# A hybrid encoder block in two-part float32: the order of high and low matmul runs in pairs of wide units

## The chip, the cores and the metric

The kernel runs on one core of a Trainium2 chip. The time is the device time of one execution in microseconds; beside it stands the span of one profiled execution.

## The reference, cut to what matters

```python
u = rmsnorm(h, g_mix)
z = u @ w_in                       # q, k, v, latents, gates: 512 tokens x 2048, one matrix
...                                # two attention branches, gated, merged, projected
gu = rmsnorm(h, g_ffn) @ w_gate_up # 2048 -> 2 x 5632
h = h + (silu(gate) * up) @ w_down # 5632 -> 2048
...                                # a second gate, an embedding, a last norm
```

All of it is float32. The change is about three of these products: part of the first matrix, gate and up, and down.

## The kernel before

**Two parts.** TensorE works on float32 in a rounded form. Each operand is split into a high part (the rounded value, a copy on ScalarE) and a low part (the rest, a subtraction on VectorE). A product is high x high, high x low and low x high. The weights' high part multiplies both parts of the activations (the high run), the weights' low part only the high part (the low run).

**Seven products in place of eight.** The three matrices are multiplied by a scheme of the Strassen-Winograd kind. The work is cut into units `v` of 128 output columns for each of the two halves; each unit has seven products, `j` = 0 to 6 (B11, T1, T4, B21, T2, B22, T3), with eight weight tiles of 128x128 each (`pairs(v)`, six in the last units). The first matrix has 10 such units, gate and up has `FF` = 44, down has 24; gate, up and down are numbered through as 68 units. Units go in pairs, a = 2q and b = 2q + 1, and their products alternate: (a,0), (b,0), (a,1), (b,1) and so on. `order(v, j)` is that position. I call the two products of one j a step.

**Wide units.** In a narrow unit the high run is 16 matmuls of 256 columns (two for each weight tile), the low run eight of 256. In a wide unit (`wide(v)`, `z_wide(v)`) one matmul of 512 columns takes the place of the two: eight of 512, then eight of 256. Wide are pairs q = 1 to 20 of gate and up, four pairs in down (q = 23, 24, 27, 28) and q = 1 to 3 of the first matrix.

**The weights' ring.** The split weights of product n lie in slot n modulo 3 of `S_HI` and `S_LO`. ScalarE's copy for n waits until product n - 3 is done, whose slot it takes, and VectorE's subtraction for n waits for that copy:

```python
act.wait_ge(s_used, n - 2)          # hi(n) on ScalarE
copy(S_HI[ring(n)][:, columns(v)], operand(v, j)).then_inc(s_hi, 1)
dve.wait_ge(s_hi, n + 1)            # lo(n) on VectorE
tt(S_LO[s][:, columns(v)], operand(v, j), S_HI[s][:, columns(v)], ALU.subtract).then_inc(s_lo, 1)
```

TensorE raises `s_used` at the end of each low run, and waits for `s_hi` before the high run and `s_lo` before the low run. In the first matrix the same semaphores are called `z_used`, `z_hi` and `z_lo`.

**What is emptied when.** A unit has four banks of PSUM, which a and b of the next pair use again (a after a, b after b). ScalarE copies partial results out (`snap_s1`, `snap_row`, `snap_s2`); VectorE adds the last ones: `gate_sum(u)` after product 5 (line 2706), `up_sum(u)` after product 6 (line 2728), the latter the one for which product 0 of unit u + 2 waits. In down the adds are `add` (line 2774), in two halves for a wide unit: `add_c11_c12` after product 5, and `add_u3` after product 6, for which the next pair waits. In the first matrix they are `z_first_sum` (line 2219) and `z_second_sum` (line 2226).

**The order on VectorE** is written out by hand, t = 0 to 13 for the 14 products of a pair, `lo(14q + t + 2)` at each t. The end of a pair in gate and up is:

```python
# t = 11: lo(b,6), t_2, gate_sum(a)
# t = 12: lo(next a,0), t_4, gate_sum(b)
# t = 13: up_sum(a), lo(next b,0)
# t =  0: up_sum(b), lo(next a,1)
```

`t_2` and `t_4` are small subtractions on hidden values (lines 2762 and 2766). The copy of ScalarE is line 1311 for every use. The loads of raw weights (SyncE's queue) wait for `s_lo` and `s_sum`, and POOL adds one block onto another with a DMA.

Of the kernel before, what the change touches and what calls it, by code (L numbers as in the profile page):

```python
# [89 lines left out]
BANK_OF = (ALPHA, GAMMA, DELTA, BETA, ALPHA, GAMMA, ALPHA)  # L90


def pairs(v):

    return 6 if v >= FF + 16 else 8


def generation(v):

    return 0 if v < FF else 1 + (v - FF) // 8  # L100


def first_unit(g):

    return 0 if g == 0 else FF + 8 * (g - 1)


def bank0(v):

    return 4 * ((v + 1) % 2)  # L110


def order(v, j):

    return 14 * (v // 2) + 2 * j + v % 2


def wide(v):

    q = v // 2  # L120
    return 0 < q < FF // 2 - 1 if v < FF else q < FF // 2 + 8 and (q - FF // 2) % 4 in (1, 2)
# [30 lines left out]
def snap_at(u, which):  # L152

    return 6 * (u // 2) + ((1, 2, 5), (3, 4, 6))[u % 2][which]


def ff_sum_at(u, which):

    return 4 * (u // 2) + 2 * which + u % 2 + 1
# [7 lines left out]
def added_at(v, which):  # L167

    return sum(10 * weight(2 * q) for q in range(FF // 2, v // 2)) + weight(v) * (2 * which + v % 2 + 1)
# [4 lines left out]
def z_wide(v):  # L174

    return 0 < v // 2 < Z_UNITS // 2 - 1
# [7 lines left out]
def z_slot(v, i):  # L184

    return ((7, 4, 5, 2), (6, 0, 1, 3))[v % 2][(i - v // 2) % 4]


def z_ring(n):

    return (n + 2) % 3
# [10 lines left out]
def build(nc, xT, pT, gains, tables, mats, w_in, w_z, w_qb, w_kvb, w_a, w_b, w_o, w_gu, w_dn, w_dn6, w_pg, w_pp,  # L202
          outT):
    with ExitStack() as ctx:
# [42 lines left out]
        ps = ctx.enter_context(nc.psum_tensor("ps", [P, 8, SEQ], F32))  # L247
# [68 lines left out]
        def flat(slot):  # L316
            return slot.rearrange("p t k c -> p (t k c)")
# [4 lines left out]
        def ff_pair(g):  # L322
            return (g - G_E + 2) % 4
# [38 lines left out]
        S_HI = [flat(w_hi[:, 0]), flat(w_hi[:, 1]), hi_2[:]]  # L362
        S_LO = [flat(w_lo[:, 0]), flat(w_lo[:, 1]), lo_2[:]]
        E_HI, E_LO = ([of[i] for i in (2, 1, 0, 1)] for of in (S_HI, S_LO))

        def as_4_by_256(slot):
            return slot.rearrange("p (t k c) -> p t k c", t=2, k=KP)
# [4 lines left out]
        def ring(n):  # L372
            return (1, 0, 2)[n % 3]
# [6 lines left out]
        def x_slot(g, j):  # L380
            s, n = (7 * g + j) % 8, 6 if g == 3 else 8
            a = arena[:, 4 * s:4 * s + 4].rearrange("p u t c -> p (u t c)")
            return a[:, 0:n * 512].rearrange("p (t k c) -> p t k c", t=2, k=n)

        X_HALF = [slice(0, 256), slice(256, 512)]
# [18 lines left out]
        def z_operand(v, j):  # L404

            return RAWS[z_slot(v, (A11, A21, A22, A12, A21, A12, A22)[j])]
# [6 lines left out]
        def z_tile(j, k):  # L413
            if j == B11_:
                return r0[:, k, :, X_HALF[0]]
            if j == B21_:
                return r1[:, k, :, X_HALF[0]]
            if j == B22_:
                return r1[:, k, :, X_HALF[1]]
            return z_turned(j)[:, :, k]  # L420
# [409 lines left out]
        def _(pe):  # L830
# [135 lines left out]

            rotary_key_group()

            def z_product(v, j):
                n = order(v, j)  # L970
                if v < 2 and j == 0:
                    pe.wait_ge(u_lo, 16)
                if v == 0:
                    if j == 1:
                        pe.wait_ge(rstd_done, 1)
                    if j == 2:
                        pe.wait_ge(kr_parts, 1)
                    if j in (T1_, T4_, T2_, T3_):
                        pe.wait_ge(zx_lo, {T1_: 2, T4_: 4, T2_: 6, T3_: 8}[j])
                elif v == 1:  # L980
                    if j < 2:
                        pe.wait_ge(emptied, j + 1)
                elif j == 0:
                    pe.wait_ge(z_acc, ff_sum_at(v - 2, UP_SUM))
                if j >= 4:
                    pe.wait_ge(z_snap, snap_at(v, j - 4))
                pe.wait_ge(z_hi, n + 1)
                bank = ps[:, bank0(v) + BANK_OF[j]]
                hi, lo = S_HI[z_ring(n)], S_LO[z_ring(n)]
                both = z_wide(v)  # L990
                fresh = j < 4
                out = bank[:, X_HALF[1 if both else 0]]
                parts = bank.rearrange("p (t c) -> p t c", t=2)
                for k in range(8):
                    w, x = hi[:, k * P:k * P + P], z_tile(j, k)
                    if both:
                        mm(parts, w, x, start=fresh and k == 0, stop=False, skip_group_check=not fresh)  # L997
                    else:
                        mm(out, w, x[:, 0], start=fresh and k == 0, stop=False, skip_group_check=not fresh)  # L999
                        mm(out, w, x[:, 1], start=False, stop=False, skip_group_check=not fresh)  # L1000
                pe.wait_ge(z_lo, n + 1)
                for k in range(8):
                    i = mm(out, lo[:, k * P:k * P + P], z_tile(j, k)[:, 0], start=False, stop=k == 7,  # L1003
                           skip_group_check=not fresh)
                i.then_inc(z_used, 1)

            for a in range(0, Z_UNITS, 2):
                for j in range(7):
                    z_product(a, j)
                    z_product(a + 1, j)  # L1010

            def first_value():
                pe.wait_ge(v_in, 16)
# [163 lines left out]
            hi, lo = as_4_by_256(S_HI[2]), as_4_by_256(S_LO[2])  # L1177
# [3 lines left out]
            i.then_inc(piece_used, 1)  # L1181


            def strassen(v, j):
                n = order(v, j)
                if j == 0 and v == 1:
                    pe.wait_ge(emptied, G_E)
                elif j == 0 and v >= 2:
                    if v < FF + 2:
                        pe.wait_ge(ff_sum, ff_sum_at(v - 2, UP_SUM))  # L1190
                    else:
                        pe.wait_ge(added, added_at(v - 2, ADD_U3))
                if j == 3 and v == 1:
                    pe.wait_ge(log_done, 4)
                    pe.wait_ge(refine, 10)
                if j >= 4:
                    if v < FF:
                        pe.wait_ge(snap, snap_at(v, j - 4))
                    else:
                        pe.wait_ge(added, added_at(v, j - 4))  # L1200
                g = generation(v)
                if v == 0:
                    pe.wait_ge(xs_lo, (7, 8, 14, 14, 15, 16, 17)[j])
                elif g and v == first_unit(g):
                    pe.wait_ge(fill_lo, 14 * (g - 1) + 2 * j + 2)
                pe.wait_ge(s_hi, n + 1)
                x, bank = x_slot(g, j), ps[:, bank0(v) + BANK_OF[j]]
                hi, lo = S_HI[ring(n)], S_LO[ring(n)]
                both = wide(v)
                fresh = j < 4  # L1210
                out = bank[:, X_HALF[1 if both else 0]]
                parts = bank.rearrange("p (t c) -> p t c", t=2)
                for k in range(pairs(v)):
                    if v == 0 and k == 6 and j >= 2:
                        pe.wait_ge(xs_lo, (18, 19, 20, 21, 22)[j - 2])
                    w = hi[:, k * P:k * P + P]
                    if both:
                        mm(parts, w, x[:, :, k], start=fresh and k == 0, stop=False, skip_group_check=not fresh)  # L1218
                    else:
                        mm(out, w, x[:, 0, k], start=fresh and k == 0, stop=False, skip_group_check=not fresh)  # L1220
                        mm(out, w, x[:, 1, k], start=False, stop=False, skip_group_check=not fresh)  # L1221
                pe.wait_ge(s_lo, n + 1)
                for k in range(pairs(v)):
                    i = mm(out, lo[:, k * P:k * P + P], x[:, 0, k], start=False, stop=k == pairs(v) - 1,  # L1224
                           skip_group_check=not fresh)
                i.then_inc(s_used, 1)

            pe.wait_ge(op_lo, OP_B + OPS_B * HEADS)
            for a in range(0, UNITS, 2):
                for j in range(7):  # L1230
                    strassen(a, j)
                    strassen(a + 1, j)
                    if a == 0 and j == 2:
                        total(3, 1)

# [2 lines left out]
            for g in range(8):  # L1238
# [5 lines left out]
                hi, lo = (of[g // 2].rearrange("p (k c) -> p k c", k=2) for of in (E_HI, E_LO))  # L1244
                c = [slice(256 * (g % 2) + P * t, 256 * (g % 2) + P * t + P) for t in range(2)]
                out = [ps[:, 2 * ff_pair(G_E + g) + t, :] for t in range(2)]
# [755 lines left out]
        def _(dve):  # L2002
# [333 lines left out]
            def seam_rotate(m, tile, before):  # L2336
                _, r, out = spare(m)
                dve.wait_ge(hnorm, m + 1)
                rotate(m, tile, 0, out, r, HD // 2, 2 * m + 2, before)
                dve.wait_ge(roped, m + 1)  # L2340
# [862 lines left out]
```

## Time and profile before

| | us |
|---|---|
| median of 3 runs (2646.85 to 2647.05) | 2646.94 |
| span of the profiled execution | 2645.5 |
| TensorE busy | 2630.8 |
| VectorE busy | 2019.1 |
| ScalarE busy | 1284.6 |

The span is one profiled execution from its first to its last instruction. In the trace a matmul stands with its full passage, so matmuls that follow each other overlap; the distance between two starts is what one costs. In a timeline row "x8" is a run of eight, and the number in brackets at a row's end is the idle time of the engine before it and what ended it.

### The profile page before, as it was taken

To read this page: it belongs to the slowest core of one execution; us is meant where nothing else is said; L and a number is where in the kernel's file an instruction comes from. 1 tells how busy PE (TensorE), PEld (TensorE's weight loads), DVE (VectorE), ACT (ScalarE), POOL (GpSimd) and SP (SyncE) were. 2 spreads that over 40 slices of the span, in tenths; PEclk is the share of its full clock that TensorE was granted. 3 is DMA by queue.
4 is the path that set the end of the run, shared out by engine and by line. 5 is a ranking of instruction groups with operands and counts; after the bars stand their busy time and mean duration, and the time that the engine had idled before them with its cause. 6 is when DMAs were issued, how large, how long until landed. Compare 5 with 4: busy or idle time off the path is not lost.

```text
span 2645.5 us, 37943 instructions
## 1 busy us (share of the span) xinstructions
PE 2630.8 (99%) x14980; PEld 2307.9 (87%) x14980; DVE 2019.1 (76%) x2314; ACT 1284.6 (49%) x1609; POOL 178.6 (7%) x140
## 2 busy tenths in 40 slices
PE   9999999999999999999999999999999999999998
PEld 7989888888888888898888888888899898999887
DVE  8887777655565433488998999999899898898745
ACT  7545455434455233455545555554555353454543
POOL 0000000010000111100000000000000000000052
PEclk9999999999999999999999999999999999999999
DMA  7545423233333554446546555545666664653332
GB/s 252 154 143 169 123 87 96 80 91 119 98 100 103 183 210 124 145 127 177 166 144 178 168 158 173 175 138 166 175 198 213 211 211 140 207 140 106 94 101 99
DMA packets 135791, 392.75 MB, mean 148 GB/s; under 512 B 11600, under 2 KB 41424, under 8 KB 133072
## 3 DMA queue, kind: packets, MB, share of 16 engines
q1 hardware_dynamic: 119904, 342.27, 38.8%
q0 software_dynamic: 11232, 39.85, 8.5%
q10 hardware_dynamic: 4496, 8.44, 0.8%
q8 instruction: 109, 1.79, 0.3%
q14 instruction: 50, 0.41, 0.0%
HBM read 304.26 MB, written 46.40 MB: 133 GB/s over the span
## 4 chain that ended last, share of the span: by engine, by line
PE 97%; DVE 2%; ACT 1%; issue 0%; DMA 0%; DVEq 0%; ACTq 0%
PE ps L1218 23%; PE ps L848 23%; PE ps L1224 16%; PE ps L853 11%; PE ps L1220 4%; PE ps L1221 4%; PE ps L997 3%; PE ps L1003 3%; PE ps L837 1%; PE ps L835 1%; PE ps L836 1%; PE ps L918 1%; PE ps L1000 1%; PE ps L999 1%; PE ps L1250 1%; PE ps L907 0%
## 5 line engine op out<-in xcount | busy, mean ns | idle before, releaser
L1311 ACT ACTIVATE w_hi<-raw 128x1024 fp32r<-128x1024 f32 (+1 forms) x538 | 562.6, 1046 | 753.5 <-PE ps L1224 409.9
L848 PE MATMUL ps<-arena,w_hi 128*128 128x512 f32 x2704 | 647.6, 391 | 0.2 <-DVE res L2038 0.2
L848 PEld LDWEIGHTS ps<-arena,w_hi 128*128 128x128 f32 x2704 | 505.3, 188 | 108.7 <-issue 3.4
L1218 PE MATMUL ps<-arena,w_hi 128*128 128x512 f32 x1792 | 448.7, 392 | 0.0
L2586 DVE TENSOR_TENSOR w_lo<-raw,w_hi 128x1024 fp32r<-128x1024 f32 (+1 forms) x314 | 373.8, 1191 | 78.8 <-ACT w_hi L1311 77.3
L2026 DVE TENSOR_TENSOR w_lo<-raw,w_hi 128x1024 fp32r<-128x1024 f32 x172 | 219.1, 1275 | 224.5 <-ACT w_hi L1311 223.6
L1218 PEld LDWEIGHTS ps<-arena,w_hi 128*128 128x128 f32 x1792 | 322.3, 189 | 57.6
L1224 PEld LDWEIGHTS ps<-arena,w_lo 128*128 128x128 f32 x2468 | 332.3, 191 | 17.5
L1224 PE MATMUL ps<-arena,w_lo 128*128 128x256 f32 x2468 | 346.4, 283 | 0.0
L853 PE MATMUL ps<-arena,w_lo 128*128 128x512 f32 x1352 | 334.3, 389 | 0.0
L1311 ACT ACTIVATE hi<-raw 128x1024 fp32r<-128x1024 f32 (+1 forms) x182 | 189.6, 1042 | 243.4 <-PE ps L1224 212.8
L853 PEld LDWEIGHTS ps<-arena,w_lo 128*128 128x128 f32 x1352 | 253.8, 188 | 52.7
L1218 PE MATMUL ps<-arena,hi 128*128 128x512 f32 x896 | 224.4, 392 | 0.0
L2586 DVE TENSOR_TENSOR lo<-raw,hi 128x1024 fp32r<-128x1024 f32 (+1 forms) x156 | 186.1, 1193 | 43.6 <-ACT hi L1311 42.8
L1218 PEld LDWEIGHTS ps<-arena,hi 128*128 128x128 f32 x896 | 161.1, 189 | 28.8
L1224 PEld LDWEIGHTS ps<-arena,lo 128*128 128x128 f32 x1228 | 165.4, 191 | 8.8
L1224 PE MATMUL ps<-arena,lo 128*128 128x256 f32 x1228 | 172.3, 283 | 0.0
L1220 PE MATMUL ps<-arena,w_hi 128*128 128x256 f32 x676 | 166.3, 283 | 0.2 <-ACT res L1311 0.2
L1221 PE MATMUL ps<-arena,w_hi 128*128 128x256 f32 x676 | 166.2, 283 | 0.0
L3065 POOL DMA_DIRECT2D raw<-raw x68 | 59.0, 868 | 1218.5 <-DMA raw<-w_gu 785.9
L1220 PEld LDWEIGHTS ps<-arena,w_hi 128*128 128x128 f32 x676 | 129.7, 192 | 0.5 <-ACT res L1311 0.4
L1221 PEld LDWEIGHTS ps<-arena,w_hi 128*128 128x128 f32 x676 | 129.8, 192 | 0.1
(280 smaller groups left out, 3360.0 us busy)
## 6 DMA issues: line engine op xcount, KB each, us to landing
raw<-w_gu SPq DMA_DIRECT2D x174, 512.0 KB, 4.1
raw<-raw POOLq DMA_DIRECT2D x70, 512.0 KB, 7.7
raw<-w_in SPq DMA_DIRECT2D x68, 512.0 KB, 3.6
raw<-w_dn SPq DMA_DIRECT2D x64, 512.0 KB, 5.3
hid<-res SPq DMA_DIRECT2D x22, 1024.0 KB, 5.0
raw<-w_z SPq DMA_DIRECT2D x40, 512.0 KB, 5.4
raw<-w_o SPq DMA_DIRECT2D x32, 512.0 KB, 3.7
raw<-w_pg SPq DMA_DIRECT2D x32, 512.0 KB, 3.6
```

The costliest lines, as they stand in the source:

```text
L848: mm(ps[:, bank + t, :], w_hi[:, s, t, k], x[:, part, :], start=first and k == 0 and part == 0, stop=False)
L853: i = mm(ps[:, bank + t, :], w_lo[:, s, t, k], x[:, 0, :], start=False, stop=last and k == len(xs) - 1)
L997: mm(parts, w, x, start=fresh and k == 0, stop=False, skip_group_check=not fresh)
L1003: i = mm(out, lo[:, k * P:k * P + P], z_tile(j, k)[:, 0], start=False, stop=k == 7, skip_group_check=not fresh)
L1218: mm(parts, w, x[:, :, k], start=fresh and k == 0, stop=False, skip_group_check=not fresh)
L1220: mm(out, w, x[:, 0, k], start=fresh and k == 0, stop=False, skip_group_check=not fresh)
L1221: mm(out, w, x[:, 1, k], start=False, stop=False, skip_group_check=not fresh)
L1224: i = mm(out, lo[:, k * P:k * P + P], x[:, 0, k], start=False, stop=k == pairs(v) - 1, skip_group_check=not fresh)
L1311: return nc.scalar.activation(out, in_, ACT.Copy, scale=scale)
L2026: tt(w_lo[:, j % HL], raw[:, j], w_hi[:, j % HL], ALU.subtract).then_inc(w_lo_done, 1)
L2586: tt(S_LO[s][:, columns(v)], operand(v, j), S_HI[s][:, columns(v)], ALU.subtract).then_inc(s_lo, 1)
L3065: pool.dma_start(RAWS[into][:, columns(v)], RAWS[more][:, columns(v)], accum_op=ALU.add).then_inc(sum_1_in[v % 2], 16)
```

## The change

In a wide pair, products 1 to 5 of both units are regrouped: high run of a, high run of b, low run of a, low run of b. Products 0 and 6, and all narrow pairs, keep their order. No matmul, copy, subtraction or load is added or removed.

```diff
+def together(both, j):
+
+    return both and 0 < j < 6
...
-            def strassen(v, j):
+            def strassen_high(v, j):
                 n = order(v, j)
...
+            def strassen_low(v, j):
+                n = order(v, j)
+                lo, x = S_LO[ring(n)], x_slot(generation(v), j)
+                out = ps[:, bank0(v) + BANK_OF[j], X_HALF[1 if wide(v) else 0]]
                 pe.wait_ge(s_lo, n + 1)
                 for k in range(pairs(v)):
                     i = mm(out, lo[:, k * P:k * P + P], x[:, 0, k], start=False, stop=k == pairs(v) - 1,
-                           skip_group_check=not fresh)
+                           skip_group_check=j >= 4)
                 i.then_inc(s_used, 1)
...
             for a in range(0, UNITS, 2):
                 for j in range(7):
-                    strassen(a, j)
-                    strassen(a + 1, j)
+                    strassen_high(a, j)
+                    if not together(wide(a), j):
+                        strassen_low(a, j)
+                    strassen_high(a + 1, j)
+                    if together(wide(a), j):
+                        strassen_low(a, j)
+                    strassen_low(a + 1, j)
                     if a == 0 and j == 2:
                         total(3, 1)
```

The same is done to `z_product` of the first matrix, split into `z_product_high` and `z_product_low` and called in the same way with `z_wide(a)`.

TensorE, step 4 of a wide pair in gate and up, before (`hi`, `w_hi` are slots of the high parts, `lo`, `w_lo` of the low parts; the first four rows are unit a):

```order
L1218 MATMUL ps<-arena,hi 128x512 [waits s_hi,snap]
L1218 MATMUL ps<-arena,hi 128x512 x7
L1224 MATMUL ps<-arena,lo 128x256 [waits s_lo]
L1224 MATMUL ps<-arena,lo 128x256 x7
L1218 MATMUL ps<-arena,w_hi 128x512 [waits s_hi,snap]
L1218 MATMUL ps<-arena,w_hi 128x512 x7
L1224 MATMUL ps<-arena,w_lo 128x256 [waits s_lo]
L1224 MATMUL ps<-arena,w_lo 128x256 x7
```

The same place on TensorE in the changed kernel:

```order
L1233 MATMUL ps<-arena,hi 128x512 [waits s_hi,snap]
L1233 MATMUL ps<-arena,hi 128x512 x7
L1233 MATMUL ps<-arena,w_hi 128x512 [waits s_hi,snap]
L1233 MATMUL ps<-arena,w_hi 128x512 x7
L1244 MATMUL ps<-arena,lo 128x256 [waits s_lo]
L1244 MATMUL ps<-arena,lo 128x256 x7
L1244 MATMUL ps<-arena,w_lo 128x256 [waits s_lo]
L1244 MATMUL ps<-arena,w_lo 128x256 x7
```

The high run of b, with its waits, stands ahead of the low run of a, whose last matmul raises `s_used` for a. The low run of b ends the step as before.

VectorE at the end of a wide pair in gate and up, before, from the subtraction for (b,6) to up_sum of b:

```order
L2586 TENSOR_TENSOR w_lo<-raw,w_hi 128x1024 [waits s_hi]
L2762 TENSOR_TENSOR res<-res 128x256 [waits t_sum]
L2706 TENSOR_TENSOR res<-res,ps 128x1024 [waits s_used,snap]
L2586 TENSOR_TENSOR lo<-raw,hi 128x1024 [waits s_hi]
L2766 TENSOR_TENSOR res<-res 128x256 [waits t_sum]
L2706 TENSOR_TENSOR res<-res,ps 128x1024 [waits s_used,snap]
L2728 TENSOR_TENSOR res<-res,ps 128x1024 [waits s_used,snap]
L2586 TENSOR_TENSOR w_lo<-raw,w_hi 128x1024 [waits s_hi]
L2728 TENSOR_TENSOR res<-res,ps 128x1024 [waits s_used,snap]
```

In the changed kernel the same rows stand in the same order with the same waits, 25 lines further down in the code. The whole orders of VectorE and ScalarE are unchanged; only TensorE's is another.

## Rows read from the trace of the kernel before

**Rows 1.** The page, busy time of TensorE and VectorE.

```profile
PE 2630.8 (99%) x14980; PEld 2307.9 (87%) x14980; DVE 2019.1 (76%) x2314; ACT 1284.6 (49%) x1609; POOL 178.6 (7%) x140
```

**Rows 2.** Busy time in stretches: pair 9, and from lo (b,2) to lo (b,6).

```profile
core 0: us, PE busy (x) PEld busy (x) DVE busy (x) ACT busy (x) POOL busy (x), PEclk, DMA share, GB/s
1483.03:1522.14 39.11, 39.11 (x227) 34.41 (x225) 35.33 (x38) 19.79 (x22) 1.75 (x2) 1.00 0.56 162
1492.77:1515.11 22.34, 22.34 (x129) 19.66 (x128) 20.18 (x22) 12.93 (x15) 1.75 (x2) 1.00 0.54 141
```

**Rows 3.** Timeline of TensorE (start, us), first matmul of pairs 1 and 21.

```profile
1170.18 0.40 PE L1218 MATMUL ps<-arena,hi 128*128 128x512 f32 x1
...
1952.31 0.28 PE L1220 MATMUL ps<-arena,w_hi 128*128 128x256 f32 x1
```

**Rows 4.** Timeline of TensorE where one width follows itself.

```profile
61.77 1.12 PE L1003 MATMUL ps<-arena,lo 128*128 128x256 f32 x8
62.73 0.28 PE L999 MATMUL ps<-arena,w_hi 128*128 128x256 f32 x1
...
2503.46 3.79 PE L848 MATMUL ps<-arena,w_hi 128*128 128x512 f32 x16
2507.09 1.75 PE L853 MATMUL ps<-arena,w_lo 128*128 128x512 f32 x7
```

**Rows 5.** Timeline of TensorE, end of pair 9: (b,5), (a,6), next pair's (a,0).

```profile
1513.76 2.00 PE L1218 MATMUL ps<-arena,hi 128*128 128x512 f32 x8
...
1516.55 2.00 PE L1218 MATMUL ps<-arena,w_hi 128*128 128x512 f32 x8
...
1522.14 0.86 PE L1218 MATMUL ps<-arena,hi 128*128 128x512 f32 x3
```

**Rows 6.** Timeline of ScalarE there: copies for (b,6) and next (a,0).

```profile
1514.02 1.06 ACT L1311 ACTIVATE w_hi<-raw 128x1024 fp32r<-128x1024 f32 x1 [1.25 <-PE ps L1224]
1516.81 1.06 ACT L1311 ACTIVATE hi<-raw 128x1024 fp32r<-128x1024 f32 x1 [1.73 <-PE ps L1224]
```

**Rows 7.** Timeline of VectorE there, t_2 and t_4 left out.

```profile
1515.11 1.23 DVE L2586 TENSOR_TENSOR w_lo<-raw,w_hi 128x1024 fp32r<-128x1024 f32 x1 [0.24 <-ACT w_hi L1311]
...
1516.59 1.22 DVE L2706 TENSOR_TENSOR res<-res,ps 128x1024 f32<-128x1024 f32 x1
1517.91 1.22 DVE L2586 TENSOR_TENSOR lo<-raw,hi 128x1024 fp32r<-128x1024 f32 x1
...
1519.38 1.21 DVE L2706 TENSOR_TENSOR res<-res,ps 128x1024 f32<-128x1024 f32 x1
1520.52 1.22 DVE L2728 TENSOR_TENSOR res<-res,ps 128x1024 f32<-128x1024 f32 x1
```

**Rows 8.** Timelines of VectorE and TensorE at the end of pair 21.

```profile
1991.94 0.68 DVE L2728 TENSOR_TENSOR res<-res,ps 128x512 f32<-128x512 f32 x1
...
1992.67 0.39 PE L1220 MATMUL ps<-arena,hi 128*128 128x256 f32 x1
1992.89 0.28 PE L1221 MATMUL ps<-arena,hi 128*128 128x256 f32 x1
```

**Rows 9.** Timelines of VectorE and TensorE, end of pair 24, in down.

```profile
2105.42 1.41 DVE L2774 TENSOR_TENSOR res<-ps,res 128x512 f32<-128x512 f32 x2
2107.07 1.23 DVE L2586 TENSOR_TENSOR lo<-raw,hi 128x1024 fp32r<-128x1024 f32 x1 [0.24 <-ACT hi L1311]
2108.21 2.86 DVE L2774 TENSOR_TENSOR res<-ps,res 128x512 f32<-128x512 f32 x4
...
2111.30 0.28 PE L1220 MATMUL ps<-arena,hi 128*128 128x256 f32 x1
```

**Rows 10.** Timelines of VectorE and TensorE, end of pair 2, first matrix.

```profile
172.50 1.22 DVE L2219 TENSOR_TENSOR res<-res,ps 128x1024 f32<-128x1024 f32 x1
174.16 1.23 DVE L2196 TENSOR_TENSOR lo<-raw,hi 128x1024 fp32r<-128x1024 f32 x1 [0.44 <-ACT hi L1311]
...
176.43 1.22 DVE L2226 TENSOR_TENSOR res<-res,ps 128x1024 f32<-128x1024 f32 x1
...
178.39 0.40 PE L997 MATMUL ps<-arena,hi 128*128 128x512 f32 x1
```

More of the change, by code:

```diff
@@ L967, in _, with z_product_high @@
             rotary_key_group()
-            def z_product(v, j):
+            def z_product_high(v, j):
                 n = order(v, j)
@@ L988, in z_product @@
                 bank = ps[:, bank0(v) + BANK_OF[j]]
-                hi, lo = S_HI[z_ring(n)], S_LO[z_ring(n)]
+                hi = S_HI[z_ring(n)]
                 both = z_wide(v)
@@ L1000, in z_product, with z_product_low @@
                         mm(out, w, x[:, 1], start=False, stop=False, skip_group_check=not fresh)
+            def z_product_low(v, j):
+                n = order(v, j)
+                lo = S_LO[z_ring(n)]
+                out = ps[:, bank0(v) + BANK_OF[j], X_HALF[1 if z_wide(v) else 0]]
                 pe.wait_ge(z_lo, n + 1)
@@ L1008, in _ @@
                 for j in range(7):
-                    z_product(a, j)
-                    z_product(a + 1, j)
+                    z_product_high(a, j)
+                    if not together(z_wide(a), j):
+                        z_product_low(a, j)
+                    z_product_high(a + 1, j)
+                    if together(z_wide(a), j):
+                        z_product_low(a, j)
+                    z_product_low(a + 1, j)
             def first_value():
@@ L1207, in strassen @@
                 x, bank = x_slot(g, j), ps[:, bank0(v) + BANK_OF[j]]
-                hi, lo = S_HI[ring(n)], S_LO[ring(n)]
+                hi = S_HI[ring(n)]
                 both = wide(v)
@@ L1221, in strassen @@
                         mm(out, w, x[:, 1, k], start=False, stop=False, skip_group_check=not fresh)
+            def strassen_low(v, j):
+                n = order(v, j)
+                lo, x = S_LO[ring(n)], x_slot(generation(v), j)
+                out = ps[:, bank0(v) + BANK_OF[j], X_HALF[1 if wide(v) else 0]]
                 pe.wait_ge(s_lo, n + 1)
@@ L1224, in strassen @@
                     i = mm(out, lo[:, k * P:k * P + P], x[:, 0, k], start=False, stop=k == pairs(v) - 1,
-                           skip_group_check=not fresh)
+                           skip_group_check=j >= 4)
                 i.then_inc(s_used, 1)
```

## The prediction

> **What bounds the kernel now.** I read the page first: TensorE is busy 99% of the span [rows 1]. Then the busy times of one pair of wide units in the gate and up product: in its 39.11 us TensorE is busy for all of it at a granted clock of 1.00, its 2.4 GHz level, while VectorE is busy 35.33 us, ScalarE 19.79 us and the DMA engines 0.56 of the time [rows 2]. So TensorE's own stream sets the time and nothing makes it wait. From the first matmul of pair 1 to the first of pair 21 are 782.13 us [rows 3], which is 20 pairs of 39.11 us, or 280 products of 2.79 us. Each pair after the first takes the same time to a hundredth, so what I find at one pair counts for its like. But VectorE is 90% full, takes its work strictly as written, and hands TensorE a bank of PSUM at each pair's start. That hand-over is the place to look at.
>
> **The seams between runs.** A wide product is eight matmuls of 512 columns (high) and eight of 256 (low). Where only one width stands, 16 matmuls of 512 take 3.63 us, so 0.227 each, and eight of 256 take 0.96 us, so 0.120 each [rows 4]. Eight of each would be 2.774 us; a product takes 2.793. The other 0.02 us goes at the changes of width. The change turns high, low, high, low into high, high, low, low: two of four width changes go, once in each of five steps of a pair. Wide pairs are 20 in gate and up, 4 in down, 3 in the first matrix: 27 x 5 = 135 steps, 135 x 0.02 = 2.7 us gained. Instructions are neither added nor taken away, and each matmul keeps its size. Between nothing (the cost belongs to each run's start, whatever stood before) and twice that, I take the 2.7.
>
> The Trainium skill ("TensorE: Matmul & The Clock Gate", section "Back-to-back issue gap") gives a spacing of N/2.4 + 2.5 ns for an isolated matmul at full clock, by its own width alone. By that rule the regrouping would gain nothing, not 2.7 us; the rows show 227 and 120 ns where it gives 216 and 109, and a seam that it doesn't have, so I go by the rows.
>
> **What the regrouping makes later.** I call a pair's first unit a and its second b, T5, T6 and T7 the starts of its products 5 and 6 and of the next pair. In step 5 the product (a,5) used to end 2.79 us before T6, since all of (b,5) followed: 1513.76 against 1516.55 [rows 5]. Now only the low run of b follows, 8 x 0.120 = 0.96 us. So `s_used` for (a,5) comes 2.79 - 0.96 = 1.83 us later against T6 and T7. The ring has three slots, and (b,6) takes the one of (a,5). ScalarE is already waiting for it: its copy for (b,6) starts at 1514.02, 0.26 us after (a,5) ends, takes 1.06 us, and it idled 1.25 us before it [rows 6]. VectorE waits for that copy too: `lo` for (b,6) starts at 1515.11 after 0.24 us of idle time [rows 7]. Both start 1.83 us later.
>
> Behind this `lo` VectorE has, in order: t_2, gate_sum of a, `lo` for the next (a,0), t_4, gate_sum of b, and last up_sum of a, without which the next pair's first matmul may not write its bank. In [rows 7] gate_sum starts at 1516.59 and `lo` at 1517.91, 1.32 us later; the same work back to back is 1.14 us (1519.38 to 1520.52), so 0.18 us is an idle piece that can absorb. up_sum of a ends at 1520.52 + 1.22 = 1521.74, and TensorE starts the next pair at 1522.14 [rows 5]: a margin of 0.40 us. The delay passes it by 1.83 - 0.18 - 0.40 = 1.25 us.
>
> What a late hand-over costs beyond that is seen once, at the end of pair 21: up_sum ends at 1991.94 + 0.68 = 1992.62, the first matmul starts at 1992.67, and the second only 0.22 us after it, where 0.12 is usual, as the weights' load no longer lies beside another matmul [rows 8]. That is 0.05 + 0.10 = 0.15 us. So each of these junctions stalls TensorE 1.25 + 0.15 = 1.40 us; 20 of them are 28.0 us.
>
> **The same in the other two stages.** In down the chain is `lo` (b,6), two halves of an add, `lo` (a,0), four halves. Idle before `lo` is 0.24 us, 0.32 with the 0.08 by which back-to-back work overlaps in the rows (1.22 long, 1.14 apart); the last half ends at 2108.21 + 2.86 = 2111.07, and TensorE goes on at 2111.30 [rows 9]: 1.83 - 0.32 - 0.23 + 0.15 = 1.43 us, four times, 5.7 us. In the first matrix there is no t_2 or t_4: `lo` starts 1.66 us after the sum where 1.13 would do, so 0.53 is absorbed, and the last sum ends at 176.43 + 1.22 = 177.65 against 178.39 [rows 10]: 1.83 - 0.53 - 0.74 + 0.15 = 0.71 us, three times, 2.1 us.
>
> **Does VectorE reach `lo` (b,6) in time, and does anything else come late?** In steps 2 to 5 only the b copies come 1.83 us later. From `lo` (b,2) to `lo` (b,6) are 22.34 us with 20.18 us of work [rows 2]; both ends move by the same, so 2.2 us of room stays. Going through the list with the work back to back, I find VectorE waiting again before `lo` (b,5), 0.9 us, and before `lo` (b,6), 1.2 us, so it is there when the copy is. TensorE now wants the high part of b earlier: copy (b,j+1) ends 0.26 + 1.06 us after (a,j), that is 0.36 us into the next step, and the high run of b begins 1.84 us into it: 1.5 us to spare. Low parts stay 3 us ahead. The copy behind a late one on ScalarE, (a,j+1), was due at 0.26 us of the step and can now start at about 0.3; copies out of PSUM that stand before it push it further, but it is wanted only at the next step, 5.6 us on, and ScalarE is idle for half of the pair. Loads are issued behind `lo`, so up to 1.8 us later; the room for them is the covering assumption that I can show least. The bank that up_sum of b frees is asked for half a product later, and that wait stays covered.
>
> **The sum.** 28.0 + 5.7 + 2.1 - 2.7 = +33.1 us. The profiled span of 2645.5 us becomes 2678.6, and the runs, whose median of 2646.94 lies 1.4 us above that span, 2680.0 us, 1.25% slower. Bounds of the unknown: without the 0.15 us it is 27 x 0.15 = 4.1 us less, 2676; if the absorbing idle pieces were already spoken for (0.18 x 20 + 0.32 x 4 + 0.53 x 3 = 6.5 us) it is 2686.5. I take the middle, since each piece has a row of its own.
>
> **Rivals.**
> - No stall. If VectorE's chain were not started by the copy of (b,6), or if the pair's slack were 1.5 us more, only the seams would count: 2646.94 - 2.7 = 2644.2, 0.1% faster, not to be told from no change. For it speaks that ScalarE is half idle. Against it, the idle 0.24 us in front of that `lo` names the copy as what it waits for, and the margin behind it is 0.40. It decides at a delay under 0.58 us (0.40 + 0.18); I have 1.83. Chance 0.05.
> - Part of the stalls absorbed, because a stall lets VectorE run ahead into the next pair. A third gone gives 2646.94 + 24 - 2.7 = 2668. Against it: the start of the chain is tied to TensorE's own (a,5), which a stall moves too. Chance 0.07.
> - Stalls are dearer. With no idle piece and no margin to absorb it each junction costs 1.83 + 0.15 = 1.98 us, 53.5 - 2.7 = +50.8, 2697.7; a load or a copy that comes late inside the pair would do this, or a wait at a second place. Half way is 2689. Chance 0.08.
> - No seam gain, as by the rule above: 35.8 us, 2682.7. Chance 0.05.
> - The forecast: 0.75.
>
> **How the numbers follow.** The forecast and the seamless rival hold 0.8, between 2676 and 2686.5. I widen to the third absorbed and to just past half way of the dear case: 2668 to 2692. A measurement of this kernel tells about 0.2%, 5.3 us, from no change. All cases but the first lie above 2652: slower 0.94, the same 0.05, faster 0.01.
>
> **What the changed profile should show.** Idle time of TensorE in front of the high run of each unit a that follows a wide pair, released by VectorE's up_sum (and its counterparts), 27 times and nowhere else new; pairs of about 40.4 us in gate and up; two high runs in 16 x 0.227 + 0.03 us; `lo` (b,6) 1.8 us later against T6, with idle time before it; up_sum of a ending 1.25 us after where T7 would be. I am wrong if VectorE isn't idle before `lo` (b,6), if the first matmul of a pair waits for something else, or if TensorE waits inside the pair.

## The result, and the profile after

The changed kernel takes 2708.45 us (median of 5 runs, 2707.98 to 2709.15) where the kernel before takes 2646.94 (5 runs): ratio 1.0232, 95% interval 1.0221 to 1.0243. That is 61.5 us slower. I had forecast 33.1 us slower and a range that ends at 2692, so the sign was right and the size was not: the time lies outside the range.

The page after, busy times and the shares of the engines in the chain of work that ended last:

```profile
span 2706.5 us, 37943 instructions
PE 2642.0 (98%) x14980; PEld 2307.8 (85%) x14980; DVE 2014.7 (74%) x2314; ACT 1272.6 (47%) x1609; POOL 178.6 (7%) x140
PE 89%; DVE 6%; ACT 2%; issue 2%; DMA 0%; DVEq 0%; ACTq 0%
```

The instructions are as many as in [rows 1], the span is 61.0 us longer. In the chain that ended last VectorE has 6% and ScalarE 2% now, where they had 2% and 1%: TensorE waits. For whom, the view of waits says, TensorE's rows alone (us in total, times, longest; L1233 is the high run of a wide unit, L1235 that of a narrow one, L1002 and L1004 are these two in the first matrix):

```profile
PE ps L1233 <- DVE res L2753: 21.7, 19, 1.4
PE ps L1233 <- ACT res L1336: 19.6, 20, 1.2
PE ps L1235 <- DVE res L2799: 2.3, 2, 1.2
PE ps L1233 <- DVE res L2799: 2.3, 2, 1.2
PE ps L1002 <- ACT res L1336: 1.6, 2, 0.8
...
PE ps L1235 <- DVE res L2753: 1.1, 1, 1.1
...
PE ps L1002 <- DVE res L2251: 0.9, 2, 0.5
PE ps L1004 <- DVE res L2251: 0.5, 1, 0.5
```

Line 2753 is `up_sum`, 2799 `add`, 2251 `z_second_sum`: these are the waits at a pair's end that I had forecast, 20 + 4 + 3 of them. Line 1336 is ScalarE's copy. The 20 waits for it in gate and up, and two in the first matrix, I had not forecast. A wide pair of gate and up, pair 9, beside the first line of [rows 2]:

```profile
core 0: us, PE busy (x) PEld busy (x) DVE busy (x) ACT busy (x) POOL busy (x), PEclk, DMA share, GB/s
1507.70:1549.37 41.67, 39.58 (x224) 34.37 (x225) 35.16 (x38) 19.36 (x23) 1.75 (x2) 1.00 0.52 152
```

41.67 us in place of 39.11, at the same granted clock (PEclk) of 1.00. TensorE's timeline of this pair shows a step without a stall (step 2), then the two stalls (in step 4, and after product 6, where the next pair starts):

```profile
1518.97 2.00 PE L1233 MATMUL ps<-arena,w_hi 128*128 128x512 f32 x8
1520.81 1.98 PE L1233 MATMUL ps<-arena,hi 128*128 128x512 f32 x8
1522.62 1.11 PE L1244 MATMUL ps<-arena,w_lo 128*128 128x256 f32 x8
1523.58 1.12 PE L1244 MATMUL ps<-arena,lo 128*128 128x256 f32 x8
...
1530.10 2.00 PE L1233 MATMUL ps<-arena,hi 128*128 128x512 f32 x8
1533.07 0.50 PE L1233 MATMUL ps<-arena,w_hi 128*128 128x512 f32 x1 [0.96 <-ACT res L1336]
...
1542.50 2.00 PE L1233 MATMUL ps<-arena,w_hi 128*128 128x512 f32 x8
...
1547.13 1.11 PE L1244 MATMUL ps<-arena,w_lo 128*128 128x256 f32 x8
1549.37 0.74 PE L1233 MATMUL ps<-arena,hi 128*128 128x512 f32 x2 [1.13 <-DVE res L2753]
```

In step 2 the first high run takes 1.84 us and the second 1.81: the seam is paid once. At 1530.10 the high run of (a,4) is followed by that of (b,4) 2.97 us later, not 1.84. The row at 1542.50 is the start of (a,6), which is T6. At 1547.13 the low run of (b,6) starts, which takes 0.95 us elsewhere, and the next pair follows 2.24 us later. VectorE there, to be laid beside [rows 7]:

```profile
1542.89 1.23 DVE L2611 TENSOR_TENSOR w_lo<-raw,w_hi 128x1024 fp32r<-128x1024 f32 x1 [1.06 <-ACT w_hi L1336]
...
1544.37 1.22 DVE L2731 TENSOR_TENSOR res<-res,ps 128x1024 f32<-128x1024 f32 x1
1545.50 1.22 DVE L2611 TENSOR_TENSOR lo<-raw,hi 128x1024 fp32r<-128x1024 f32 x1
...
1548.10 1.22 DVE L2753 TENSOR_TENSOR res<-res,ps 128x1024 f32<-128x1024 f32 x1
```

The subtraction for (b,6) starts 0.39 us after T6 (1542.50), where it started 1.44 us before it: 1.83 us later. It waited 1.06 us for the copy. `up_sum` of a starts at 1548.10, ends at 1549.32, and TensorE starts at 1549.37. This is the chain as forecast. The other stall is in the chain that ended last, from 1529.40 to 1533.07:

```profile
1529.40 1.07 ACT w_hi L1336
...
1531.64 0.69 DVE res L2778
...
1532.42 0.61 ACT res L1336
...
1533.07 0.50 PE ps L1233
```

These are ScalarE's copy for (b,4) (late, since (a,3) is released late), VectorE's `lo` for (b,4) and behind it `hidden_tile` of unit a - 2 (line 2778, the product of the unit's gate and up values), ScalarE's `snap_s1` of b (the copy of product 0's bank out of PSUM), and then the high run of (b,4). `snap_s1` of b waits for `hidden_tile` of a - 2, because the rows that it fills are a ring of three units, and that product is their last reader. And product 4 of a unit adds onto the bank of product 0, so it waits for that copy. In the kernel before, `snap_s1` of b ended 1.8 us into the step and was wanted at 2.79; now it ends 2.93 us into it (1533.03) and is wanted at 1.84.

### The profile page after: what moved, and what is told of

It reads as the page before. It is cut to its first block, busy times and chain, and to the rows that moved or that the text cites. A ratio compares the mean times of both kernels' runs of the same rounds, so it can differ in the third digit from the quotient of the medians.

```text
span 2706.5 us, 37943 instructions
## 1 busy us (share of the span) xinstructions
PE 2642.0 (98%) x14980; PEld 2307.8 (85%) x14980; DVE 2014.7 (74%) x2314; ACT 1272.6 (47%) x1609; POOL 178.6 (7%) x140
## 4 chain that ended last, share of the span: by engine, by line
PE 89%; DVE 6%; ACT 2%; issue 2%; DMA 0%; DVEq 0%; ACTq 0%
PE ps L853 22%; PE ps L1233 20%; PE ps L1244 14%; PE ps L858 11%; PE ps L1235 4%; PE ps L1236 4%; PE ps L1002 2%; PE ps L1013 2%; PE ps L842 1%; PE ps L840 1%; PE ps L841 1%; PE ps L923 1%; ACT w_hi L1336 1%; PE ps L1004 1%; PE ps L1005 1%
## 5 line engine op out<-in xcount | busy, mean ns | idle before, releaser
L1233 PE MATMUL ps<-arena,w_hi 128*128 128x512 f32 x1792 | 444.6, 393 | 28.6 <-DVE res L2753 14.9
L1233 PEld LDWEIGHTS ps<-arena,w_hi 128*128 128x128 f32 x1792 | 326.0, 188 | 98.5 <-ACT res L1336 18.0
L1244 PE MATMUL ps<-arena,w_lo 128*128 128x256 f32 x2468 | 340.3, 283 | 0.0
L1244 PEld LDWEIGHTS ps<-arena,w_lo 128*128 128x128 f32 x2468 | 324.6, 191 | 11.5
L858 PEld LDWEIGHTS ps<-arena,w_lo 128*128 128x128 f32 x1352 | 253.8, 188 | 52.7
L1233 PE MATMUL ps<-arena,hi 128*128 128x512 f32 x896 | 225.0, 393 | 15.0 <-ACT res L1336 7.0
L1233 PEld LDWEIGHTS ps<-arena,hi 128*128 128x128 f32 x896 | 163.0, 188 | 50.1 <-ACT res L1336 10.0
L1235 PE MATMUL ps<-arena,w_hi 128*128 128x256 f32 x676 | 166.6, 283 | 2.5 <-DVE res L2799 1.2
L1235 PEld LDWEIGHTS ps<-arena,w_hi 128*128 128x128 f32 x676 | 129.7, 192 | 3.2 <-DVE res L2799 1.4
```

The source lines that it names most:

```text
L858: i = mm(ps[:, bank + t, :], w_lo[:, s, t, k], x[:, 0, :], start=False, stop=last and k == len(xs) - 1)
```

## The experiments

The theory from here on: two separate chains, each started by the late release of a unit's ring slot, one before (b,4) and one at a pair's end, and beside them the seams' 2.7 us. Its rivals are that VectorE is simply too full for the regrouped order, so that each regrouped step costs a share of the 61.5 us, and that the stall before (b,4) comes from the earlier demand alone.

**One step, or some of the steps.** Four kernels differ from the changed one in one line:

```diff
 def together(both, j):
 
-    return both and 0 < j < 6
+    return both and j == 5         # e1; e2: 0 < j < 5; e3: 0 < j < 4; e4: j == 4
```

> Only step 5 of each wide pair is regrouped. Theory (two separate chains): the stall at a pair's end comes from the late release of (a,5) alone, so it stays whole, 20 x 1.42 + 4 x 1.45 + 3 x 0.75 = 36.5 us, and the stall before (b,4) is gone; seams give back 27 x 0.02 = 0.5: 2682.9 us. Rival (VectorE is simply too full, so each regrouped step costs its share): 61.5 / 5 = 12.3 us, 2659.

> Steps 1 to 4 are regrouped, step 5 is not. Theory: no stall at a pair's end; the stall before (b,4) stays, 20 x 1.29 + 2 x 1.14 + 0.14 = 28.2 us, less 108 x 0.02 = 2.2: 2672.9 us. Rival (each step its share): 4 x 12.3, 2696.

> Steps 1 to 3 are regrouped. (a,3) is still released late, but the high run of (b,4) is wanted 2.79 us into its step and not 1.84. Theory (late release and early demand add up): the copy snap_s1 of b ends 2.9 us into the step, so about 0.25 us of stall is left in 22 pairs, +5.5, less 1.6: 2650.8 us. Rival (early demand alone makes the stall before (b,4)): 2646.9 - 1.6 = 2645.3. Rival (each step its share): 2683.

> Only step 4 is regrouped: (b,4) is wanted early, but (a,3) is released as before. Theory (late release and early demand add up): snap_s1 of b ends 1.81 us into the step as before, and TensorE wants it at 1.72: a stall of about 0.2 us, 23 times, +4.6, less 0.5: 2651 us. Rival (early demand alone): 20 x 1.29 + 2.4 = 28.2, 2674.6. Rival (each step its share): 2659.

| steps regrouped | expected | measured (before: 2646.86) | ratio, 95% interval |
|---|---|---|---|
| 5 | 2682.9 | 2682.60 | 1.0135, 1.0118 to 1.0152 |
| 1 to 4 | 2672.9 | 2679.55 | 1.0123, 1.0106 to 1.0140 |
| 1 to 3 | 2650.8 | 2653.79 | 1.0027, 1.0017 to 1.0038 |
| 4 | 2651 | 2654.80 | 1.0029, 1.0018 to 1.0041 |

TensorE's waits with step 5 alone:

```profile
PE ps L1233 <- DVE res L2753: 21.7, 19, 1.4
PE ps L1233 <- DVE res L2799: 2.3, 2, 1.2
PE ps L1235 <- DVE res L2799: 2.3, 2, 1.2
PE ps L1235 <- DVE res L2753: 1.1, 1, 1.1
```

With steps 1 to 4:

```profile
PE ps L1233 <- ACT res L1336: 19.6, 20, 1.2
PE ps L1235 <- DVE res L2799: 2.1, 2, 1.4
PE ps L1002 <- ACT res L1336: 1.6, 2, 0.8
...
PEld ps L1233 <- DVE res L2753: 3.0, 19, 0.2
```

PEld is TensorE's weight load. Step 5 alone brings 35.7 us and the waits at the pairs' ends, to the tenth the same as in the changed kernel. Steps 1 to 4 bring the waits for `snap_s1`; of those at the ends of pairs in gate and up only a short one of the weight load is left. A share for each step is out: one step costs 36 us and three cost 7.

Steps 1 to 3 release (a,3) as late as the changed kernel does, and step 4 alone asks for (b,4) as early. Distances between starts tell what each costs at (b,4) itself, in most of the 20 pairs: 0.29 us with steps 1 to 3, 0.16 with step 4, 1.27 in the changed kernel. So late release and early demand use up the same room together, as expected.

All but the first came out 3 to 7 us above, and the two halves, 35.7 and 32.7 us, make 6.9 more than the whole. The distances between starts show both. With step 4 regrouped and step 5 not, TensorE starts each of the 20 pairs after a wide one 0.12 us late and loses 0.11 more in its first product, 4.5 us that I had not counted and that the long stall covers where step 5 is regrouped too. Steps 1 to 4 lose another 2.2 us in two stalls in down. Steps 1 to 3 lose 1.3 us there, for which see the last experiments. In step 4 alone the profiled execution has 0.9 us more in the first pair of the first matrix, where nothing is regrouped.

**Each chain cut by itself.** On VectorE `hidden_tile` goes ahead of the subtraction (e5), then on ScalarE `snap_s1` of b ahead of the copy for (a,5) as well (e6):

```diff
+                    if q != FF // 2 and last and t == 7:
+                        hidden_tile(a - 2)
                     if 14 * q + t + 2 < 7 * UNITS:
                         lo(14 * q + t + 2)
...
                         if t == 7:
-                            hidden_tile(a - 2)
                             gate_fold(b - 2)
...
+                    if t == 8 and now:
+                        snap_s1(b)
                     if 14 * q + t + 2 < 7 * UNITS:
                         hi(14 * q + t + 2)
...
                     if t == 8 and now:
-                        snap_s1(b)
                         snap_row(b)
```

> The changed kernel, and on VectorE the product hidden_tile of unit a - 2 stands ahead of the subtraction lo for (b,4) and not behind it. Theory (the stall before (b,4) in gate and up is the chain copy (b,4), lo (b,4), hidden_tile, snap_s1 of b): hidden_tile no longer waits for the late copy, and only ScalarE's own order is left, copy (b,4), copy (a,5), snap_s1, whose end is 1.9 us into the step: stall 0.2 to 0.3 in place of 1.29, 20 x 1.0 = 20 us off, 2688. Rival (ScalarE's order alone makes that stall): 2708, no change.

> As the run before, and on ScalarE snap_s1 of b stands ahead of the copy for (a,5). Theory: the stall before (b,4) in gate and up is gone: 2708.45 - 20 x 1.29 = 2682.6. Rival (VectorE is too full, its work has to go somewhere): a stall of like size at another place, 2700 or more.

At the pair's end `up_sum` of a goes ahead of `gate_sum` of b, and `up_sum` of b ahead of `lo` (e7; the counts of `ff_sum` follow the new order):

```diff
-                    if t == 0:
-                        (up_sum if last else add_u3)(b - 2)
-                    if t == 13:
-                        (up_sum if now else add_u3)(a)
...
+                    if t == 13 and now:
+                        gate_sum(b)
+                        up_sum(b)
...
                         if t == 12:
-                            gate_sum(b)
+                            up_sum(a)
```

> The changed kernel, and VectorE ends a pair of gate and up in the order gate_sum a, lo (next a,0), t_4, up_sum a, gate_sum b, up_sum b, lo (next b,0), so that one piece of 1.13 us less stands ahead of each up_sum. Theory (the stall at a pair's end is the length of the chain behind copy (b,6)): up_sum a ends 1.13 us earlier, stall 1.42 - 1.13 = 0.29 or a little less: 20 x 1.13 = 22.6 off, 2685.9. Rival (VectorE's total work bounds the pair): no change, 2708.

Measured beside 2647.09 for the kernel before: e5 2686.46 (1.0149, 1.0133 to 1.0166), e6 2683.81 (1.0140, 1.0123 to 1.0157), e7 2685.68 (1.0146, 1.0129 to 1.0162). Expected were 2688, 2682.6 and 2685.9. TensorE's waits in e5:

```profile
PE ps L1233 <- DVE res L2753: 21.7, 19, 1.4
PE ps L1233 <- DVE res L2799: 2.3, 2, 1.2
PE ps L1235 <- DVE res L2799: 2.3, 2, 1.2
PE ps L1002 <- ACT res L1336: 1.6, 2, 0.8
PE ps L1235 <- DVE res L2753: 1.1, 1, 1.1
```

and in e7, whose lines lie five further down:

```profile
PE ps L1238 <- ACT res L1341: 19.6, 20, 1.2
PE ps L1238 <- DVE res L2804: 2.3, 2, 1.2
PE ps L1240 <- DVE res L2804: 2.3, 2, 1.2
PE ps L1007 <- ACT res L1341: 1.6, 2, 0.8
```

Moving one subtraction of 1.13 us behind `hidden_tile` takes away the 20 waits for line 1336 and 22 us; moving one addition of 1.13 us behind `up_sum` takes away the long waits for `up_sum`, down to 0.26 us a pair, and 22.8 us. Each leaves the other's waits untouched to the tenth. VectorE does the same work in all three, so it isn't too full; what it does first decides.

**The late copy without any regrouping** (e8), in the kernel before:

```diff
+                elif wide(v) and v % 2 and j == 6:
+                    act.wait_ge(s_used, n - 1)
                 else:
                     act.wait_ge(s_used, n - 2)
```

> The kernel before, TensorE's order untouched; only ScalarE's copy for (b,6) of a wide pair in gate, up and down waits one product longer, for (b,5) in place of (a,5). Theory (the stall at a pair's end is the late copy and nothing of the regrouping): the copy starts 2.79 us later, 2.79 - 0.18 - 0.40 + 0.15 = 2.36 us for each of 20 pairs, 2.79 - 0.32 - 0.23 + 0.15 = 2.39 for each of 4 in down: +56.8, 2703.8 us. Rival (the stall comes from the order of the runs on TensorE): no change, 2646.9.

Measured 2715.64 (2711.59 to 2719.63) beside 2646.95, ratio 1.0256 (1.0240 to 1.0271). TensorE waits there for `up_sum`, which is line 2730 in this kernel:

```profile
PE ps L1218 <- DVE res L2730: 39.9, 19, 2.4
```

In the profiled execution 19 of the 20 junctions of gate and up come 2.25 us late and one 2.53, and where the clock stays up 0.12 us more goes in the next product: the 2.36 expected. So the stall at a pair's end needs nothing but a late copy. The 12 us above the expectation are something else, told in the last section.

**Both chains cut, and the seams left.** Steps 1 and 2 touch neither chain (e9). e10 is TensorE's old order with the reorderings of e6 and e7 (and t_2 and t_4 behind `up_sum` of a). e11 has them with the regrouping of all steps in gate and up and of steps 1 and 2 elsewhere:

```diff
-def together(both, j):
+def together(both, j, end=3):
 
-    return both and 0 < j < 6
+    return both and 0 < j < end
...
-                    if not together(wide(a), j):
+                    if not together(wide(a), j, 6 if a < FF else 3):
...
-                    if together(wide(a), j):
+                    if together(wide(a), j, 6 if a < FF else 3):
```

> Steps 1 and 2 alone are regrouped. Theory: no wait is touched, only the seams count, 27 x 2 x 0.02 = 1.1 us off: 2645.8. Rival (each regrouped step costs its share, 12.3 us): 2671. Rival (no seam gain, as the page's spacing by width alone has it): 2646.9.

> The kernel before in TensorE's order, with the reorderings on the other engines alone: hidden_tile ahead of lo (b,4), snap_s1 of b ahead of the copy for (a,5), and on VectorE gate_sum a, lo (next a,0), up_sum a, t_2, t_4, gate_sum b, up_sum b, lo (next b,0) at the end of a pair. Theory: TensorE waited for nothing there, so nothing changes, 2646.9. A rival: the reordering makes a wait of its own, above 2650.

> All five steps regrouped in gate and up, steps 1 and 2 alone in down and in the first matrix, together with the reorderings of the run before. Theory: both chains fit again, only the seams are left, 20 x 5 x 0.02 + 7 x 2 x 0.02 = 2.3 us off: 2644.6. Rival (VectorE is too full for the regrouped order): stalls of 0.3 us or more in each of 20 pairs, 2651 or more.

Measured beside 2646.95 (27 runs): e9 2648.74 (1.0007, 0.9998 to 1.0016), e10 2647.34 (1.0000, 0.9991 to 1.0010), e11 2648.44 (1.0005, 0.9996 to 1.0014). The 61 us are gone, but the medians of e9 and e11 lie 1.5 to 1.8 us above the kernel before, not 1.1 to 2.3 below. The intervals of the ratios span both signs, so by them alone no difference is shown; but ten of e9's eleven runs are longer than the longest of the 27. In e9's profiled execution the starts say where: gate and up are 0.7 us shorter than before, down is 1.8 us longer. ScalarE's waits for loads in down (2010 us to 2460) in e9:

```profile
ACT hi L1336 <- DMA raw<-w_dn: 8.6, 3, 4.2
ACT w_hi L1336 <- DMA raw<-w_dn: 3.8, 2, 2.5
```

and in e11:

```profile
ACT hi L1341 <- DMA raw<-w_dn: 11.2, 3, 6.4
ACT w_hi L1341 <- DMA raw<-w_dn: 5.2, 3, 2.0
```

The kernel before has no such row in that stretch. But e10, where TensorE's order is the old one, has 6.8 us of them, and TensorE waits for none. In e9 it does. One of four places where the chain that ended last passes over a load:

```profile
2058.14 1.15 DVE lo L2611
...
2059.31 7.76 DMA raw<-w_dn
...
2067.09 1.07 ACT w_hi L1336
```

It does so in e2, e3 and e11 too, and nowhere in down in e1, e4, e10, the changed kernel or the kernel before. So it is the regrouping of steps 1 and 2 there that brings TensorE to wait for loads, where the stalls of step 5 don't hold it back anyway. In e11's timelines a copy waits 6.36 us for its load, and TensorE then 3.33 us. This profiled execution is the slowest of e11's eleven, 5.3 us above their median, so the stall is not typical:

```profile
2155.08 1.06 ACT L1341 ACTIVATE hi<-raw 128x1024 fp32r<-128x1024 f32 x1 [6.36 <-DMA raw<-w_dn]
...
2158.05 0.58 PE L1240 MATMUL ps<-arena,hi 128*128 128x256 f32 x1 [3.33 <-DVE res L2805]
```

Two more kernels keep down and the first matrix in the old order (`end=1`, and `3 if a < FF else 1` for e12, `6 if a < FF else 1` with the reorderings for e13).

> Steps 1 and 2 regrouped in gate and up alone; down and the first matrix as before, nothing reordered. Theory (what the run with steps 1 and 2 everywhere lost was lost in down, to loads of raw weights that land later): 40 x 0.02 = 0.8 us off, 2646.1. Rival (it was lost to the regrouping as such, in gate and up too): 2648 or more.

> All five steps regrouped in gate and up alone, with the reorderings on VectorE and ScalarE. Theory: 100 x 0.02 = 2.0 us off, of which short waits of 0.07 before (b,4) give back 1.2: 2646.1, and no single long wait in down. Rival (the regrouping in gate and up shifts loads as well): 2648 or more, with a wait for a load in the trace.

Measured beside 2647.26 (21 runs, 2646.89 to 2647.99): e12 2646.45 (2646.07 to 2647.04), ratio 0.9997, 0.9988 to 1.0006; e13 2646.70 (2646.01 to 2647.20), 0.9997, 0.9988 to 1.0006. The medians are 0.8 and 0.6 us below, but the interval of the ratio spans both signs: a gain in time isn't shown by it. The starts in the profiled executions do show the seams: gate and up are 0.78 us shorter in e12 than before, 0.02 in each of 40 steps. In e13 100 steps give 2.0 us, and about 0.06 us in each pair before (b,4) and 0.13 at one end take 1.3 back. So the regrouping in gate and up costs nothing once its chains fit, and e9 lost its time in down. e12 and e13 have 5.5 and 6.5 us of ScalarE waiting for loads in down too, and no stall of TensorE from them.

What the regrouping does to the loads in down can be read in part. They are issued behind `lo`, and `lo` of b comes late: in e9 three loads in each wide pair there are issued 0.7 to 1.8 us later against the load ahead of them. In pair 27 they start from 2215.30 us where the kernel before has 2212.53, 2.77 us later, while the load ahead of them is issued 0.97 later. The ones behind them then take longer, up to 9.2 us where it was 4.8 before and 6.1 in e12. Why they take longer was not tried apart, and stays open.

## Why the prediction was right and wrong

- **What bounds the kernel, and the seams: right.** TensorE's stream set the time, and a merged pair of high runs takes 1.84 + 1.81 us, with 0.95 + 0.96 for the low runs: 0.02 us saved in each step. The starts of e12 moved by the same 0.02 in each step; its time moved by 0.8 us, which its interval can't tell from nothing.
- **The chain at a pair's end: right, in each stage.** Forecast were 1.40, 1.43 and 0.71 us for gate and up, down and first matrix. The distances between starts in the changed kernel give 1.29 + 0.12, 1.32 + 0.10 and 0.62 + 0.10 us, where the second number is what the next product is longer. All 27 are 36.2 us, with 0.27 more in one of them, against 35.8 in the sum. e1 measured 35.7 by itself, after the 0.5 us that its seams give back. e8 shows that the late copy is the cause, e7 that the order of VectorE behind it is the price.
- **"Does anything else come late?": wrong.** This is the step that failed. I wrote that the copy for b has 1.5 us to spare, and took that for all that the high run of b waits for. That holds for `s_hi`. But the order's rows in the section on the change have `[waits s_hi,snap]` on the high run of (b,4), and I never followed `snap` back. It leads over `snap_s1` of b to `hidden_tile` of a - 2, which stands on VectorE right behind the subtraction that I had myself made 1.83 us later, and TensorE asks for the result 0.96 us earlier. The sum had nothing for it. Measured are 1.13 us before the run and 0.14 within it, over the 20 pairs 25.6 us with 0.27 more in one. In the first matrix the same run waits 1.0 us in two pairs, behind the sigmoid and the copy for (a,5) on ScalarE, 2.4 us with the small ones. 33.1 + 25.6 + 2.4 = 61.1, against 61.5 measured. That TensorE waits inside the pair was one of my own signs of being wrong.
- **Of the rivals "stalls are dearer" had the right mechanism,** "a wait at a second place", and 0.08. Its number, 2697.7, was 10.8 us short. My bound for it, 50.8 us, was the delay paid in full at one place. Two places each cost their own.
- **The loads:** I named them the assumption that I could show least. In down of e9 they are issued up to 1.8 us later. In the changed kernel the chain that ended last passes over no load there; in e2, e3, e9 and e11 it does, and in e9 down is 1.8 us longer for it.
- The rule of the Trainium skill that would have had no seam gain ("TensorE: Matmul & The Clock Gate", section "Back-to-back issue gap") is not borne out by the timeline, and the measurement decides: 1.84 against 1.81 us for two equal runs that differ in what stood before them.

## What to carry to other kernels

When a stream without gaps is reordered, list for each run both its new demand time and its new release time, and for every semaphore in its wait list, not only the one that the edit is about, follow the releaser back to see if it stands behind something that the same edit makes late. An engine that takes its work in order and is 90% busy need not be the bound: here moving one piece of 1.13 us on it in each pair was worth 22 us, with the same work. And a gain of 0.02 us per step can't pay for a wait anywhere, so the room of every wait that the edit touches has to be read first.

## What the runs showed of the hardware

A stall can cost more than its length. In e8 TensorE waits 2.09 us at 1209.7 to 1211.8, and after it the granted clock (PEclk, third from the end) falls: the stretches before, from 1213 to 1216, and after:

```profile
1206.00:1213.00 7.00, 4.91 (x29) 4.19 (x28) 7.00 (x9) 2.33 (x3) 0.00 (x0) 1.00 0.64 203
1213.00:1216.00 3.00, 3.00 (x13) 2.69 (x12) 2.12 (x2) 0.00 (x0) 0.00 (x0) 0.51 0.17 54
1216.00:1220.00 4.00, 4.00 (x22) 3.43 (x22) 2.64 (x3) 2.27 (x3) 0.00 (x0) 0.94 0.00 0
```

0.51 is close to the lower of the two levels, 1.2 GHz of 2.4. A low run of eight then takes 1.71 us in place of 0.95. In this profiled execution it happened behind nine of the 24 stalls, at 1.5 us each, and not behind the others of about the same length. Of the 70.6 us by which its span is longer than before, the 24 stalls with the loss in the next product are 57, and the nine falls of the clock the rest. The mean clock of the four runs of e8 was 0.992 to 0.995, where the kernel before has 0.998 or 0.999. That is where its 12 us above the expectation lie. Over the stalls of 1.3 us of the changed kernel the clock stayed at 1.00. In e11 it stood at 0.50 from 2157.1 to 2162.5 us, from within the wait of 3.33 us on.
